# Mixing stage of the first two layers of a three-layer kernel: new order, VectorE sums in PSUM, tanh gates, and one GpSimd instruction per unit

## What is computed

```python
h = rmsnorm(x, g_mix);  proj = h @ w_in
gate_pre, a_in, na_qkv, dil_qkv, swa_q, swa_kv = split(proj)
y_a = silu(layernorm(depthwise_conv31(a * sigmoid(g))))      # a, g = halves of a_in
y_b, y_c, y_d = three attentions over q, k normalised per head (c, d with rope)
branch = einsum(stack(y_a..y_d), w_branch)                    # 4 x (256 -> 1024)
gates  = sigmoid(gate_pre + gate_b)
x = x + sum(gates * branch, over 4) @ w_out
x = x + conv_ffn(rmsnorm(x, g_ffn))
```

## Time and profile before

| | us |
|---|---|
| median of 3 runs | 1579.03 |
| the profiled execution's own time | 1578.67 |
| its span, first to last instruction | 1576.9 |
| TensorE matmuls busy in the span | 1501.1 (95%) |
| VectorE / ScalarE / GpSimd busy | 875.2 / 835.3 / 1220.7 |
| first layer's mixing stage | 16.8 to 280.2 |
| second layer's mixing stage | 478.4 to 740.5 |
| third layer | 938.8 to the end |

### The profile page before, as it was taken

How to read it: one execution, slowest core, us unless ns; L and a number is a source line. 1 busy time by engine, 2 the same in 40 slices (tenths; PEclk the granted TensorE clock), 3 DMA queues, 4 the chain that set the end, 5 groups by cost and what they waited for, 6 DMA issues and landing times.

```text
span 1576.9 us, 32619 instructions
## 1 busy us (share of the span) xinstructions
PE 1501.1 (95%) x10984; PEld 1404.4 (89%) x10984; DVE 875.2 (56%) x1432; ACT 835.3 (53%) x1287; POOL 1220.7 (77%) x926
## 2 busy tenths in 40 slices
PE   8997989999999998999999999898999999999998
PEld 8987877999989997787999989898989899899997
DVE  4987668544445796767444459674266364222223
ACT  5434545655555435445655565575545444655454
POOL 5974649699987875557999978787857598798985
PEclk9999999999999999999999999999999999999999
DMA  7643434465665543434565655554534455466553
GB/s 255 185 128 113 128 101 160 145 193 188 184 184 177 155 137 106 125 107 147 180 193 186 185 190 175 156 160 135 176 118 134 118 178 185 148 194 186 189 179 104
DMA packets 69790, 251.73 MB, mean 160 GB/s; under 512 B 7632, under 2 KB 10192, under 8 KB 69200
## 3 DMA queue, kind: packets, MB, share of 16 engines
q1 hardware_dynamic: 68848, 245.72, 50.4%
q10 hardware_dynamic: 864, 4.92, 0.9%
HBM read 249.56 MB, written 1.05 MB: 159 GB/s over the span
## 4 chain that ended last, share of the span: by engine, by line
PE 81%; DVE 12%; issue 4%; ACT 2%; DMA 0%; POOL 0%; DVEq 0%; SPq 0%; ACTq 0%; POOLq 0%
PE psum L740 25%; PE psum L741 24%; PE psum L742 24%; DVE arena L1312 2%; DVE arena L1445 1%; PE psum L881 1%; DVE arena L1504 1%; PE psum L844 1%; DVE mixf L1448 1%; DVE arena L1441 1%; PE psum L858 1%; PE psum L926 1%; PE psum L917 1%; DVE arena L1389 1%; PE psum L873 1%
## 5 line engine op out<-in xcount | busy, mean ns | idle before, releaser
L316 POOL TENSOR_TENSOR w_lo<-raw,w_hi 128x512 fp32r<-128x512 f32 x461 | 614.3, 1332 | 339.9 <-ACT w_hi L341 334.0
L740 PE MATMUL psum<-h_hi,w_hi 128*128 128x256 f32 x2456 | 707.0, 288 | 19.3 <-DVE small L1510 14.5
L741 PE MATMUL psum<-h_hi,w_lo 128*128 128x256 f32 x2456 | 698.8, 285 | 0.0
L742 PE MATMUL psum<-h_lo,w_hi 128*128 128x256 f32 x2456 | 698.3, 284 | 0.0
L317 POOL TENSOR_TENSOR w_lo<-raw,w_hi 128x512 fp32r<-128x512 f32 x461 | 631.7, 1370 | 0.0
L341 ACT ACTIVATE w_hi<-raw 128x1024 fp32r<-128x1024 f32 x461 | 482.0, 1052 | 74.4 <-PE psum L742 68.2
L740 PEld LDWEIGHTS psum<-h_hi,w_hi 128*128 128x128 f32 x2456 | 474.8, 193 | 30.2 <-issue 18.9
L741 PEld LDWEIGHTS psum<-h_hi,w_lo 128*128 128x128 f32 x2456 | 475.0, 193 | 2.8
L742 PEld LDWEIGHTS psum<-h_lo,w_hi 128*128 128x128 f32 x2456 | 474.8, 193 | 0.0
L740 PE MATMUL psum<-w_hi,f_hi 128*128 128x512 f32 x336 | 134.2, 399 | 7.7 <-DVE f_lo L1246 7.7
L1465 DVE SCALAR_TENSOR_TENSOR pre<-psum,prm,pre 128x255 f32<-128x255 f32 x88 | 42.5, 483 | 172.3 <-ACT pre L497 172.3
(11 more groups left out here) (264 smaller groups left out, 1885.9 us busy)
## 6 DMA issues: line engine op xcount, KB each, us to landing
raw<-in_units SPq DMA_DIRECT2D x461, 512.0 KB, 3.6
arena<-in_consts ACTq DMA_DIRECT2D x1, 2320.0 KB, 9.3
arena<-in_bias ACTq DMA_DIRECT2D x2, 1024.0 KB, 4.9
arena<-in_consts SPq DMA_DIRECT2D x1, 1657.0 KB, 7.5
out<-arena SPq DMA_DIRECT2D x4, 256.0 KB, 2.6
pre<-in_x SPq DMA_DIRECT2D x2, 256.0 KB, 3.9
arena<-in_x SPq DMA_DIRECT2D x2, 256.0 KB, 4.3
prm<-in_params ACTq DMA_DIRECT2D x2, 153.5 KB, 2.6
```

The costliest lines, as they stand in the source:

```text
L316: pool.tensor_tensor(w_lo[s][:, 0:D // 2], raw[s][:, 0:D // 2], w_hi[s][:, 0:D // 2].bitcast(F32), ALU.subtract)
L740: pe.matmul(out, hi, r_hi, start=start, stop=False, **kw)
L741: pe.matmul(out, lo, r_hi, start=False, stop=False, **kw)
L742: return pe.matmul(out, hi, r_lo, start=False, stop=stop, **kw)
```

## The change

What it does, part by part:

1. **GpSimd:** `low` is one instruction of 1024 columns instead of two of 512, for all 461 units.
2. **VectorE's operands:** the 31 taps add in PSUM bank 3 (L1329, L1334 of the changed file); scores, rope, normalisation and the gated sum keep one operand in PSUM.
3. **q, k, v and gates go to ScalarE:** ScalarE copies q and k with their gain, copies v, and applies `tanh(0.5 z + 0.5 b)` straight from PSUM to each of the 32 gate tiles. `mix` then uses `(tanh + 1) * branch` and a factor 0.5, so that the sigmoid passes over 1024 columns fall away.
4. **TensorE's order:** the sums of squares and rope partners stand between the q/k units, the spread between the v units; each attention piece is spread over five gate units (the last has six behind it); the softmax is scaled after the product with v, so that the product is token-major (64 columns) and has to be turned back (`turn_outputs`); the layernorm of the convolution moves to pieces 2 to 5.
5. **Branch phase:** four branch units first, then output and branch units alternating; the first output unit starts the sum, so `zero_acc` falls away here. The PSUM slots of a branch unit are freed at the end of `mix`, not after its first instruction. The weights are loaded in that order (`BRANCH_ORDER`).

The diff, cut to its core:

```diff
-                pool.tensor_tensor(w_lo[s][:, 0:D // 2], raw[s][:, 0:D // 2], w_hi[s][:, 0:D // 2].bitcast(F32), ALU.subtract)
-                pool.tensor_tensor(w_lo[s][:, D // 2:D], raw[s][:, D // 2:D], w_hi[s][:, D // 2:D].bitcast(F32), ALU.subtract)\
+                pool.tensor_tensor(w_lo[s][:, :], raw[s][:, :], w_hi[s][:, :].bitcast(F32), ALU.subtract)\
                     .then_inc(lo_ready, d.inc(lo_ready))
...
+def tap(i):
+    for k in range(2):
+        u = a1("u", k * (T + TAPS - 1) + i, T)
...
+        dve.scalar_tensor_tensor(a1("conv", k * T, T) if last else bank(3, k * T, T), u, prm[:, w:w + 1], bank(3, k * T, T), ALU.mult, ALU.add)
...
+def turn_scores(p, h):
+    pe.wait_ge(exp_ready, d.next(exp_ready))
...
+                for p in range(len(PIECES)):
+                    more = p + 1 < len(PIECES)
+                    fill()
+                    turn_scores(p, 0)
+                    fill()
+                    pe.wait_ge(pts_ready, d.next(pts_ready))
+                    turn_scores(p, 1)
...
+                    attend(p, 0)
+                    if more:
+                        scores(p + 1)
+                    fill()
+                    pe.wait_ge(pts_ready, d.next(pts_ready))
+                    attend(p, 1)
+                    fill()
+                    turn_outputs()          # waits for VectorE's on_ready
+                    fill()
...
+                def mix(c):
...
+                    dve.scalar_tensor_tensor(part, gat[:, 0:512], 1.0, one, ALU.add, ALU.mult).then_inc(vec, d.inc(vec))
+                    dve.scalar_tensor_tensor(two, gat[:, 512:1024], 1.0, two, ALU.add, ALU.mult).then_inc(vec, d.inc(vec))
+                    dve.wait_ge(d.last, d.made(d.last))
+                    dve.tensor_tensor(part[:, T:2 * T], two[:, T:2 * T], part[:, T:2 * T], ALU.add).then_inc(vec, d.inc(vec))
+                    dve.tensor_tensor(two[:, 0:T], two[:, 0:T], part[:, 0:T], ALU.add).then_inc(vec, d.inc(vec))
+                    dve.wait_ge(d.last, d.made(d.last))
+                    dve.tensor_tensor(two[:, 0:T], two[:, 0:T], part[:, T:2 * T], ALU.add).then_inc(mixf_ready, d.inc(mixf_ready))
+                    dve.wait_ge(fhi_ready, d.next(fhi_ready))
+                    dve.scalar_tensor_tensor(chunk(y_lo, CH + c), two[:, 0:T], 0.5, chunk(y_hi, CH + c).bitcast(F32), ALU.mult, ALU.subtract)
+                    dve.sem_inc(slot_free, d.inc(slot_free, 2))
...
+                for c in range(LAG + 1):
+                    branch_unit(act_free if c < 2 else slot_free)
+                for c in range(LAG + 1, CH):
+                    out_unit(c - LAG - 1)
+                    branch_unit(slot_free)
+                for c in range(CH - LAG - 1, CH - 2):
+                    out_unit(c)
+                last_two(y_hi, y_lo, 2 * CH - 2, flo_ready)
```

More of the change, by code:

```diff
@@ L44 @@
 SWA_TILE = 8
+BRANCH_AT = (0, 1, 2, 4, 6, 8, 10, 12)
+OUT_AT = (3, 5, 7, 9, 11, 13, 14, 15)
+BRANCH_ORDER = [*BRANCH_AT[:LAG + 1]] + [k for c in range(CH - LAG - 1) for k in (OUT_AT[c], BRANCH_AT[c + LAG + 1])] + [*OUT_AT[CH - LAG - 1:]]
 PIECES = [
@@ L283, in _ @@
             for layer in range(DEPTH):
-                first, end = max(2 * RING, layer * UNITS1), (layer + 1) * UNITS1
+                at = layer * (UNITS1 + PAD1)
+                mixed = UNITS_BEFORE + 4 * CH
+                done = 0 if layer else 2 * RING
+                order = list(range(mixed)) + [mixed + k for k in BRANCH_ORDER]
+                for u in range(done, len(order)):
+                    load(at + order[u], (layer * UNITS1 + u) % RING)
+                first, end = layer * UNITS1 + len(order), (layer + 1) * UNITS1
                 ahead = -first % RING
@@ L373, in norm, with exps @@
                 high(ahead)
-            def exps(p):
+            def exps(p, h):
                 q_tile = PIECES[p][0]
[L377 to L391, removed]
@@ L474, in feed_high @@
+                high()
+                gate()
                 def feed_high(b):
@@ L885, in _, with turn_outputs @@
+                if h:
+                    last.then_inc(o_ready, d.inc(o_ready))
+            def turn_outputs():
+                pe.wait_ge(on_ready, d.next(on_ready))
+                for r in range(2):
+                    last = pe.transpose(bank(3, T + r * P, P), rows_of_y[:, r * P:(r + 1) * P], ident)
+                last.then_inc(yt_ready, d.inc(yt_ready))
             pe.wait_ge(init, d.next(init))
@@ L931, in partners @@
-                def partners(tiles, b):
-                    for j in tiles:
-                        last = pe.matmul(bank(b, j % 2 * T, T), ck("perm", 0, P), a1("qk", j * T, T), start=True, stop=True)
-                    last.then_inc(pm_ready, d.inc(pm_ready))
-                pe.wait_ge(qr_ready, d.next(qr_ready))
-                spread(range(8))
-                for _ in range(RING):
-                    linear_unit(h_hi, h_lo, free=gate_free)
-                pe.wait_ge(qn_ready, d.next(qn_ready, 8))
@@ L954, in _ @@
-                for k in range(2):
-                    last = pe.matmul(bank(1, 0, T), ones256, a1("conv", k * T, T), start=(k == 0), stop=(k == 1))
-                last.then_inc(mean_ready, d.inc(mean_ready))
-                for _ in range(2):
-                    linear_unit(h_hi, h_lo, free=gate_free)
-                pe.wait_ge(sq_ready, d.next(sq_ready))
-                for k in range(2):
-                    last = pe.matmul(bank(1, T, T), ones256, a1("sg", k * T, T), start=(k == 0), stop=(k == 1))
```

549 lines of the change are left out of this document (279 added, 270 removed).

## The result

The changed kernel takes 1559.96 us (median of 4 runs, 1558.34 to 1560.48), the kernel before 1579.16 us beside it (4 runs, 1578.85 to 1586.46). The ratio is 0.9866 with a 95% interval of 0.9837 to 0.9895: 1.3% faster, 6 us above the forecast of 1554 us and inside its range. The profiled execution has a time of 1560.48 us and a span of 1558.7 us.

The account below looks back on a forecast made before the run. TensorE was taken as the bound, held up in the mixing stages by VectorE, slowed through sharing with GpSimd. From 1578.67 us, minus 29.6 in the mixing stages, plus 5 for the long instruction: 1554 us, own range 1545 to 1565.

Parts of the forecast that it names:

- the start: Start of each mixing stage: waits for w_lo (3.0 us) and convolution input (1.1) stay in the first layer; 2 in the second.
- The third and fourth branch unit: Branch phase: each waits 0.9 us for PSUM slots freed at the end of `mix`, 1.9 us per layer.
- The four small instructions: Two attention pieces: VectorE's SBUF-only instructions meet GpSimd's, delaying `turn_outputs`; 2 us a layer, between 0 and 8.
- the slow clock: Mixing stages: granted clock 0.86 around the 5.9 us wait for the last convolution tap; both would go.
- Pace and entries: TensorE per mixing stage: bare pace 236.3 us, plus 4.2 us for entries after about 42 small groups.
- The long instruction: One GpSimd instruction per unit makes VectorE's SBUF-only instructions wait in the third layer: 5 us more, between 0 and 10.
- in the feed-forwards ... hidden: Feed-forwards: low part due only some 17 us after its units, so the long GpSimd instruction costs nothing there.
- D: Rival: GpSimd becomes the bound from 2.95 us an instruction; at 3.1, 92 us more over 461 units, 1646 us; chance 0.04.
- the taps in PSUM: Mixing stages: all 31 taps with a PSUM operand take 0.47 instead of 1.2 us, removing the 5.9 us wait.
- A: Rival: everything hidden, products at 0.11 us, no long-instruction cost, no late small instruction; 1534 us; chance 0.18.
- B: Rival: each piece has a new wait of about 1.3 us before `turn_outputs` or transposes; 15.6 us more, 1570; chance 0.14.
- C: Rival: the lock makes 25 third-layer instructions each wait a further 1.3 us, 33 us instead of 5; 1582 us; chance 0.05.

Follow-up runs that it names:

- e11: Changed kernel with 16 further fast matmuls of zeros after the fourth unit of the first layer: 1559.11 us, ratio 0.9865.
- e8: Changed kernel with GpSimd's low part in three instructions of 352, 352 and 320 columns: 1546.62 us, ratio 0.9771.
- e2: Changed kernel with GpSimd's low part in four instructions of 256 columns: 1576.79 us, ratio 0.9968.
- e1: Changed kernel with GpSimd's low part in two instructions of 512 columns again: 1549.73 us, ratio 0.9805.
- e5: Changed kernel, one GpSimd instruction kept, with the convolution taps adding in SBUF as before: 1569.66 us, ratio 0.993.
- e6: Changed kernel with two GpSimd instructions of 512 columns and the convolution taps adding in SBUF: 1563.97 us, ratio 0.9898.
- e3: Changed kernel with one GpSimd instruction per unit in the first two layers, two halves in the third: 1553.86 us, ratio 0.9826.
- e10: Changed kernel with two GpSimd halves, plus four matmuls of zeros ahead of each group of spread matmuls: 1559.5 us, ratio 0.9871.

## Why the prediction was right, point by point

**The mixing stages** came to 26.5 us less, forecast 29.6. The product takes 0.20 to 0.23 us a matmul, taken at 0.22. Taps take 0.48 us, as taken. The terms of the sum that were off nearly cancel, and that is luck:

- Waits were allowed 8.5 us in the first layer and 6.4 in the second; TensorE's waits add up to 5.5 and 3.4. I had read all 3.0 us for w_lo as the start, though one of the two waits, 0.7 us before and 0.9 after, stands in the branch phase. So the start is 2.1 + 1.1 us and 1.1, not 4.1 and 2. The third and fourth branch unit come 1.04 and 0.65 us late, forecast 1.9 together. The four small instructions, for which I allowed 2 us a layer, cost nothing: `turn_outputs` never waits, and the one wait in the pieces is 0.46 us for ScalarE (L403).
- The clock was left out. I let the slow clock vanish with the 5.9-us wait. It went there, but stretches at 1.2 GHz came at 22.2, 90.5, 530.8 and 537.6 us, each about 1.5 us: 3 us a layer. The stretch at 560.1 us of the kernel before, with no wait ahead of it, could have told me.
- Pace and entries together, forecast 240.5 us a layer, come to about 242.

**The long instruction** cost 7.2 us in the third layer and 0.6 in each feed-forward, forecast 5 and nothing. TensorE's waits in the third layer grew by 5.3 us (by 3.3 in e11); of the remaining 1.9 us, 1.5 are the slow stretch at 1233.9, which the kernel before has not. So the mechanism and the size hold. The waits were not half as many, each twice as long, but 27 instead of 42, each 1.54 instead of 0.82 us. They also fell elsewhere than I said: the line of the old L1510 grew from 14.5 to 16.1 us, not to 19, and the rest is spread over others. The step "in the feed-forwards ... hidden" was wrong by 1.2 us: I looked at the weights' low part only, and left out the one VectorE instruction on the path, which meets the lock once.

**GpSimd** took 2.43 us a unit, below the 2.5 to 2.7 forecast; D had its threshold about right (from 2.95 us on): e8 at 2.87 pays nothing, e2 at 3.06 does. Its price was too high: I had each of the 461 units pay, which at 3.06 us would be 83 us, and e2 stands 27 us above e1: most of it in the feed-forwards, where units follow one another, and next to nothing in the first mixing stage (255.0 against 256.2 us), where small matmuls between the units give GpSimd time.

**Where I was right for a reason of the wrong weight.** I gave the win to the taps in PSUM. By e5 and e6 they carry 5 to 14 us, since in the new order a tap in SBUF would have cost 0.80 us, not 1.2. The rest is the order of TensorE and what is scaled when; that remainder was not taken apart further. And I booked tanh as a saving of ScalarE's passes, hidden. The step failed to ask what the gates beside the exponentials cost with another function: 29.7 us, more than the whole gain.

**The rivals.** A (all hidden, 1534) would have needed products at 0.11 us. B did not come: no wait of more than half a us in the pieces. C did not come: not 33 us but 5 to 7. Added up, the mixing stages missed by 3.1 us, the third layer by 2.2 and the feed-forwards by 1.2: 1554.1 us forecast for the profiled execution, 1560.48 measured.

## What to carry to other kernels

Where two engines exclude each other for a whole instruction, its length is a trade: shorter pieces shorten each wait of the other engine, until their own cost per instruction (0.2 us on GpSimd here) makes their engine the bound; measure one, two, three, four before choosing. Count waits per instruction of the other engine, not per instruction of your own, and look whether it rests in between. When gates and exponentials are interleaved, look first at whether their functions need a table load between them. And when two versions differ by less than some 3 us in one stage, look at where each trace has its slow stretches, and at a stretch of the program that both share, before giving the difference a cause.

## What the hardware showed that I had not expected

- The granted clock fell to 1.2 GHz in stretches of 3.4 us throughout which TensorE was busy, after small float32 matmuls and no wait (at 90.5 and 530.8 us). The same instructions had such a stretch in one trace and not in another (84.8 us in e3, 90.5 in the changed kernel). In e10 matmuls of zeros among the small ones did not remove it.
- Two engines excluding each other cost VectorE nothing while GpSimd rested: taps at 0.47 us in between. A run of 18 such taps held a GpSimd instruction up in its turn: 5.35 us instead of 2.39.
- GpSimd's time is 2.43, 2.64, 2.87 and 3.06 us for the same 1024 columns in one, two, three and four instructions.
- A table load holds ScalarE for 1.28 us, and the next activation follows at once.
